# A two-layer decoder trunk in split fp32r: three of eight row-block pairs of the down products by seven products, in a new order

## The chip, the cores and the metric

The kernel runs on one core of a Trainium2 chip. The metric is the device time of one execution in microseconds (us). The core has a matrix engine (TensorE), a vector engine (VectorE), an activation engine (ScalarE), GpSimd, a queue of loads (SyncE) and 16 DMA engines. In the rows of the profile they are called PE (its weight loads PEld), DVE, ACT, POOL, SP. Each runs its own instructions in program order and waits on semaphores for the others.

## The reference

256 tokens of width 2048 pass through a gated mixer, a feed-forward block, an attention block and a second feed-forward block, all in float32. The change lies in the two feed-forward blocks:

```python
def swiglu_ffn(x, norm_g, w_gate, w_up, w_down):
    h = rms_norm(x, norm_g)                                   # 256 x 2048
    return (jax.nn.silu(h @ w_gate) * (h @ w_up)) @ w_down    # 5632 hidden columns
```

`x` and the result are 256 x 2048, `w_gate` and `w_up` 2048 x 5632, `w_down` 5632 x 2048.

## The kernel before

**Split products.** Each float32 matrix is written as hi + lo in the matrix engine's format fp32r. One product of a 128x128 block with 128x512 weights is three matmuls: hi by hi (L1609), hi by lo (L1610), lo by hi (L1611). ScalarE makes w_hi by a copy (L741). VectorE makes w_lo as raw - w_hi (`plain_lo`, L1160). Some half groups are "added" (table `ADDED`): ScalarE writes -raw to w_lo as well (L743), and GpSimd starts a transfer that adds raw to it in memory (L541), so VectorE has nothing to do for them.

**Half groups and pairs.** The 16 row blocks of a product are eight row-block pairs, numbered 0 to 7. For two column groups g and u (512 columns each) the plain way takes two half groups, g3 and u3 for instance, of 4 products (12 matmuls) each. The other way (`s0`) is a two-by-two block product in Winograd's form: 7 products (21 matmuls) in place of 8, over sums of blocks. `pair_sums` on VectorE (L1149, L1152, L1155, tile sums_b) forms the sums of the weights, `pair_hi` on ScalarE (L730) makes the three parts of s_hi, `pair_lo` on VectorE (L1165, L1168, L1171) the three parts of s_lo. The matrix engine waits for the first part (`blocks_split`) at the pair's start, and for the others 9 and 15 matmuls on. The left side's sums (`forms_begin`, `forms_next`, `forms_end`, `forms_hi_part`, `forms_lo_part`) are made once for a block.

**Stages.** The hidden columns go in parts (`PARTS`) of 4, 4 and 3 chunks. After the chunks of parts 0 and 1 come two blocks, "down 0" and "down 1", of two column groups each: 4 of each in the program. The third part has two plain columns and a "down middle" block.

**Order and memory.** `ORDERS` is written by hand and fixes the items' order on all engines; `ACT_ORDERS` is ScalarE's own where that differs. `LOADS` says which half groups share a load of 1 MB. A load goes to one of four slots of `raw`, in turn, and `slot_free` makes the load queue wait until the load four before it has been split: for a half group until w_lo is written, for an added one until its transfer is done, for a pair until s_lo is. w_hi and w_lo are rings of four half groups: ScalarE may write one when the matrix engine has used the one four before. s_hi and s_lo exist once; a part is rewritten when the pair before has used it. `hooks` are pieces of other work behind an item: `gate_sums` and `hidden` end the chunk before, `hidden_lo` (L983) splits its last columns.

Of the kernel before, what the change touches and what calls it, by code (L numbers as in the profile page):

```python
# [49 lines left out]
def yoco_kernel(nc, x, a_norm, a_w_in, a_ln_g, a_ln_b, a_w_s, a_b_s, a_w_out, kv_norm, w_k, w_v, k_norm,  # L50
# [24 lines left out]
    WINO, WINO_H = 4, 2  # L75
# [5 lines left out]
    def loads_of(text):  # L81
# [6 lines left out]
              "down 0": items("g2 g3 g4 g5 u2 u3 g6 g7 s0 u4 u5 s1 u6 u7"),  # L88
              "down 1": items("g2 g3 g4 g5 g6 g7 s0 u2 u3 u4 u5 s1 u6 u7"),
# [3 lines left out]
             "down 0": loads_of("g2 g3,g4 g5,u2 u3,g6 g7,s0,u4 u5,s1,u6 u7"),  # L93
             "down 1": loads_of("g2 g3,g4 g5,g6 g7,s0,u2 u3,u4 u5,s1,u6 u7"),
# [121 lines left out]
    with ExitStack() as ctx:  # L216
# [18 lines left out]
        junk_b = sb("junk_b", [P, CH], mybir.dt.bfloat16)  # L235
# [32 lines left out]
        with ExitStack() as part:  # L268
# [9 lines left out]
            f4_hi = sb("f4_hi", [P, WINO - 2, P], F32R, part)  # L278
            f4_lo = sb("f4_lo", [P, WINO - 2, P], F32R, part)
# [31 lines left out]
        def in_place(rows, first=0):  # L311
            return rows[:, first:first + 4:2, P:2 * P]
# [246 lines left out]
        def _(act):  # L559
# [187 lines left out]
            def forms_hi_part(n, dst, fourth, rest=None):  # L747

                act.wait_ge(forms_ready, n)
                pairs_n = dst.shape[1]  # L750
# [4 lines left out]
                ins.then_inc(forms_hi, 1)

            def feed_forward(layer, norm, last_save, last_lhs):
# [34 lines left out]
                for p, (c0, c1) in enumerate(PARTS):  # L792
                    for c in range(c0, c1):
                        k = layer, "chunk", c
                        if c == 0:
# [10 lines left out]
                    if p in DOWN_PAIRS:  # L806
                        block_hi((layer, "down", p, 0),
                                 {("g", 3): [lambda: read_p1(k)], ("g", 4): [lambda: silu(c1 - 1)],
                                  ("u", 2): [lambda: hidden_hi(c1 - 1, c0)],
                                  ("u", 3): [lambda: forms_hi_part(FORMS[layer, "down", p, 0], fh_hi, in_place(h_hi))]})  # L810
                        block_hi((layer, "down", p, 1), {("g", 3): [lambda: read_p1((layer, "down", p, 0))]})
                        continue
# [15 lines left out]
                    middle = {("g", 2): [lambda: forms_hi_part(FORMS[km], fh_hi, in_place(h_hi, h_spare(p)))]}  # L828
# [120 lines left out]
        def _(dve):  # L949
# [213 lines left out]
            def pair_lo(n, slot):  # L1163
# [708 lines left out]
```

## Time and profile before

| | us |
|---|---|
| median of 3 runs | 2074.83 (2074.07 to 2074.86) |
| the profiled execution | 2074.55 |
| its span, first to last instruction | 2072.8 |
| TensorE busy | 2065.6 (100%) |
| VectorE busy | 1672.9 (81%) |
| ScalarE busy | 1208.1 (58%) |

The rows carry times from the start of the span. A matmul's row shows 0.39 us, but the matmuls overlap, and the distance from one start to the next is what a matmul costs. VectorE's and ScalarE's rows overlap a little too, by about 0.1 us; lengths are therefore read from start to start.

### The profile page before, as it was taken

What the parts mean: (1) busy time and instruction counts of PE and PEld (TensorE: products, weight loads), DVE (VectorE), ACT (ScalarE), POOL (GpSimd) and SP (SyncE); (2) the same over time, 40 slices, a digit from 0 to 9 for tenths busy, and PEclk for the clock granted to TensorE, in tenths of its full rate; (3) what the DMA queues carried; (4) which work ended last, traced back from release to release, by engine and by line L of the source; (5) the groups of instructions that cost most, each with busy time, mean ns of one, the idle gap of its engine ahead of it and who ended that gap; (6) DMA issues with size and microseconds to landing.
All of it is one profiled execution on the core that took longest, in us unless ns stands there. A gap on an engine that the chain in (4) does not pass through costs nothing.

```text
span 2072.8 us, 24481 instructions
## 1 busy us (share of the span) xinstructions
PE 2065.6 (100%) x9394; PEld 1714.7 (83%) x9394; DVE 1672.9 (81%) x1847; ACT 1208.1 (58%) x1452; POOL 93.2 (4%) x107
## 2 busy tenths in 40 slices
PE   9999999999999999999999999999999999999999
PEld 8888888888888888888888888878888888888887
DVE  5466579999899998988566666579999899998987
ACT  6444556665566655656666665466665566655653
POOL 1000001000000000000011001001000000000000
PEclk9999999999999999999999999999999999999999
DMA  8655547875687767765555455447866687767764
GB/s 326 206 179 175 174 159 236 259 226 197 199 269 228 231 215 212 241 210 203 195 184 168 147 187 174 163 143 240 266 214 208 194 273 219 241 207 213 241 216 150
DMA packets 212255, 434.66 MB, mean 210 GB/s; under 512 B 9040, under 2 KB 9648, under 8 KB 211888
## 3 DMA queue, kind: packets, MB, share of 16 engines
q1 hardware_dynamic: 202720, 398.50, 57.5%
q0 software_dynamic: 9424, 34.65, 8.1%
q8 instruction: 74, 1.21, 0.2%
q14 instruction: 37, 0.30, 0.0%
HBM read 399.56 MB, written 2.10 MB: 194 GB/s over the span
## 4 chain that ended last, share of the span: by engine, by line
PE 97%; DVE 1%; ACT 1%; DMA 1%; issue 0%; POOL 0%; DVEq 0%; POOLq 0%; ACTq 0%
PE acc L1609 18%; PE acc L1610 18%; PE acc L1611 18%; PE acc L1468 11%; PE acc L1472 11%; PE acc L1470 11%; PE tr L1610 2%; PE tr L1609 2%; PE tr L1611 2%; PE tr L1516 1%; DMA w_lo<-raw 1%; PE tr L1789 0%; PE tr L1579 0%; PE tr L1763 0%; PE tr L1773 0%; PE acc L1525 0%
## 5 line engine op out<-in xcount | busy, mean ns | idle before, releaser
L741 ACT ACTIVATE w_hi<-raw 128x1024 fp32r<-128x1024 f32 x320 | 328.0, 1053 | 180.4 <-PE acc L1611 160.7
L1160 DVE TENSOR_TENSOR w_lo<-raw,w_hi 128x1024 fp32r<-128x1024 f32 x260 | 308.1, 1219 | 24.1 <-ACT w_hi L741 24.1
L1609 PE MATMUL acc<-w_hi,a_hi 128*128 128x512 f32 x736 | 288.2, 392 | 1.5 <-DVE w_lo L1160 1.3
L1611 PE MATMUL acc<-w_hi,a_lo 128*128 128x512 f32 x736 | 286.6, 389 | 0.0
L1610 PE MATMUL acc<-w_lo,a_hi 128*128 128x512 f32 x736 | 286.4, 389 | 0.0
L730 ACT ACTIVATE s_hi<-sums_b 128x1024 fp32r<-128x1024 f32 x208 | 213.0, 1054 | 97.9 <-DVE sums_b L1155 90.5
L1468 PE MATMUL acc<-w_hi,a_hi 128*128 128x512 f32 x640 | 254.7, 398 | 0.0
L1472 PE MATMUL acc<-w_hi,a_lo 128*128 128x512 f32 x640 | 249.7, 390 | 0.0
L1470 PE MATMUL acc<-w_lo,a_hi 128*128 128x512 f32 x640 | 249.2, 389 | 0.0
L961 DVE TENSOR_TENSOR w_lo<-raw,w_hi 128x1024 fp32r<-128x1024 f32 x127 | 154.9, 1237 | 116.1 <-ACT w_hi L579 116.0
L730 ACT ACTIVATE s_hi<-raw 128x1536 fp32r<-128x1536 f32 x104 | 154.5, 1486 | 140.6 <-PE acc L1611 140.6
L965 DVE SCALAR_TENSOR_TENSOR w_lo<-raw,gains,w_hi 128x512 fp32r<-128x512 f32 x192 | 134.5, 748 | 83.8 <-ACT w_hi L583 83.7
L579 ACT ACTIVATE w_hi<-raw 128x1024 fp32r<-128x1024 f32 x127 | 132.2, 1058 | 117.0 <-PE acc L1472 115.8
L1165 DVE TENSOR_TENSOR s_lo<-raw,s_hi 128x1536 fp32r<-128x1536 f32 x104 | 182.4, 1754 | 20.0 <-ACT s_hi L730 20.0
L1609 PE MATMUL acc<-w_hi,h_hi 128*128 128x512 f32 x448 | 174.7, 390 | 0.0
L1611 PE MATMUL acc<-w_hi,h_lo 128*128 128x512 f32 x448 | 174.3, 389 | 0.0
L1610 PE MATMUL acc<-w_lo,h_hi 128*128 128x512 f32 x448 | 174.3, 389 | 0.0
L1609 PEld LDWEIGHTS acc<-w_hi,a_hi 128*128 128x128 f32 x736 | 138.2, 188 | 30.3 <-issue 1.7
L1611 PEld LDWEIGHTS acc<-w_hi,a_lo 128*128 128x128 f32 x736 | 138.2, 188 | 28.9
L1610 PEld LDWEIGHTS acc<-w_lo,a_hi 128*128 128x128 f32 x736 | 138.2, 188 | 28.1
L583 ACT ACTIVATE w_hi<-raw,gains 128x512 fp32r<-128x512 f32 x192 | 126.1, 713 | 60.5 <-PE acc L1472 60.4
L1472 PEld LDWEIGHTS acc<-w_hi,a_lo 128*128 128x128 f32 x640 | 120.1, 188 | 25.5
(225 smaller groups left out, 3903.5 us busy)
## 6 DMA issues: line engine op xcount, KB each, us to landing
raw<-in_ffn_w_down_dram SPq DMA_DIRECT2D x68, 1024.0 KB, 5.1
raw<-in_ffn_w_gate_dram SPq DMA_DIRECT2D x46, 1024.0 KB, 5.6
raw<-in_ffn_w_up_dram SPq DMA_DIRECT2D x46, 1024.0 KB, 6.6
raw<-in_ffn_w_gate_dram SPq DMA_DIRECT2D x84, 512.0 KB, 4.0
raw<-in_ffn_w_up_dram SPq DMA_DIRECT2D x84, 512.0 KB, 5.4
raw<-in_a_w_in_dram SPq DMA_DIRECT2D x30, 1024.0 KB, 5.3
w_lo<-raw POOLq DMA_DIRECT2D x60, 512.0 KB, 8.2
raw<-in_ffn_w_down_dram SPq DMA_DIRECT2D x40, 512.0 KB, 5.1
```

The costliest lines, as they stand in the source:

```text
L730: nc.scalar.activation(s_hi[:, operands, :], src, ACT.Copy).then_inc(s_cast, 1)
L741: ins = nc.scalar.activation(w_hi[:, m % RING, :, :], src, ACT.Copy)
L961: nc.vector.tensor_tensor(lo, src, hi, ALU.subtract).then_inc(lo_split, 1)
L965: ins = nc.vector.scalar_tensor_tensor(out=lo[:, k, :], in0=src[:, k, :], scalar=gains[:, gain + kb:gain + kb + 1], in1=hi[:, k, :], op0=A ...
L1160: nc.vector.tensor_tensor(w_lo[:, m % RING, :, :], raw[:, slot, half * HG:(half + 1) * HG, :], w_hi[:, m % RING, :, :].bitcast(F32), ALU.s ...
L1165: nc.vector.tensor_tensor(s_lo[:, 0:3, :], raw[:, slot, 1:4, :], s_hi[:, 0:3, :].bitcast(F32), ALU.subtract)\
L1468: nc.tensor.matmul(acc[s][t][:, :], hi[:, kb, tok], w_hi[:, slot, k, :], start=kb == 0, stop=False)
L1470: nc.tensor.matmul(acc[s][t][:, :], hi[:, kb, tok], w_lo[:, slot, k, :], start=False, stop=False)
L1472: ins = nc.tensor.matmul(acc[s][t][:, :], lo[:, kb, tok], w_hi[:, slot, k, :], start=False, stop=kb == HG * n - 1)
L1609: nc.tensor.matmul(bank[:, :], hi, rhs_hi, start=start, stop=False)
L1610: nc.tensor.matmul(bank[:, :], hi, rhs_lo, start=False, stop=False)
L1611: return nc.tensor.matmul(bank[:, :], lo, rhs_hi, start=False, stop=stop)
```

## The change

`WINO_H` goes from 2 to 3, so pair 2 of a down block is done by seven products as well. The orders and loads of down 0 and down 1 are new, three half groups of each down 0 (g3, g4, u7) are added ones, and the hooks are hung elsewhere. Three small tiles are gone (junk_b and the two of f4): f4 now lies in the down blocks' forms, from which `place_fourth` copies it into a_hi and a_lo, and `save_chunk` writes its squares into `res` before the copy.

```diff
-    WINO, WINO_H = 4, 2
+    WINO, WINO_H = 4, 3
...
-              "down 0": items("g2 g3 g4 g5 u2 u3 g6 g7 s0 u4 u5 s1 u6 u7"),
-              "down 1": items("g2 g3 g4 g5 g6 g7 s0 u2 u3 u4 u5 s1 u6 u7"),
+              "down 0": items("g3 g4 g5 u3 u4 u5 s0 g6 s1 g7 s2 u6 u7"),
+              "down 1": items("g3 g4 g5 g6 s0 g7 u7 s1 u3 u4 s2 u5 u6"),
...
-             "down 0": loads_of("g2 g3,g4 g5,u2 u3,g6 g7,s0,u4 u5,s1,u6 u7"),
-             "down 1": loads_of("g2 g3,g4 g5,g6 g7,s0,u2 u3,u4 u5,s1,u6 u7"),
+             "down 0": loads_of("g3 u3,g4 g5,u4 u5,g6 g7,s0,u6 u7,s1,s2"),
+             "down 1": loads_of("g3 g4,g5 g6,s0,g7 u7,s1,u3 u4,s2,u5 u6"),
...
-    ADDED = {"chunk": items("g7 u4 u5"), "first": [], "down 0": [], "down 1": [], "down middle": []}
-    ACT_ORDERS = {"chunk": items("g4 g5 g6 g7 s0 u4 s1 u5 s2 s3 u6 u7")}
+    ADDED = {"chunk": items("g7 u4 u5"), "first": [], "down 0": items("g3 g4 u7"), "down 1": [], "down middle": []}
+    ACT_ORDERS = {"chunk": items("g4 g5 g6 g7 s0 u4 s1 u5 s2 s3 u6 u7"),
+                  "down 0": items("g3 g4 g5 u3 u4 u5 s0 g6 s1 g7 u7 s2 u6")}
...
+            def place_fourth(k):
+                act.wait_ge(w_used, HG_OF[k, ("u", 3)] + 1)
+                act.wait_ge(forms_hi, FORMS[k])
+                act.wait_ge(forms_lo, FORMS[k])
+                nc.scalar.activation(in_place(a_hi, 4), f4_hi.bitcast(F32), ACT.Copy)
+                nc.scalar.activation(in_place(a_lo, 4), f4_lo.bitcast(F32), ACT.Copy).then_inc(fourth_placed, 1)
...
-                        block_lo(k0, {("g", 3): [lambda: gate_sums(c1 - 1)], ("g", 4): [lambda: hidden(c1 - 1)],
-                                      ("g", 5): [lambda: dve.wait_ge(staged, b0 + c1 - NC),
-                                                 lambda: forms_begin(h_hi, h_lo, WINO_H, PAIRS_BEFORE[k0])],
-                                      ("u", 2): [lambda: forms_next(WINO_H), lambda: forms_end(WINO_H)],
-                                      ("u", 3): [lambda: hidden_lo(c1 - 1, c0),
-                                                 lambda: forms_lo_part(FORMS[k0], fh_hi, fh_lo, in_place(h_hi), in_place(h_lo))],
-                                      ("g", 7): [lambda: dve.wait_ge(forms_lo, FORMS[k0]), lambda: sums(k0, 0)], ("u", 5): [lambda: sums(k0, 1)]})
+                        block_lo(k0, {("g", 4): [lambda: gate_sums(c1 - 1)], ("g", 5): [lambda: hidden(c1 - 1)],
+                                      ("u", 3): [lambda: dve.wait_ge(staged, b0 + c1 - NC),
+                                                 lambda: forms_begin(h_hi, h_lo, WINO_H, PAIRS_BEFORE[k0])],
+                                      ("u", 4): [lambda: forms_next(WINO_H), lambda: forms_end(WINO_H)],
+                                      ("u", 5): [lambda: forms_lo_part(FORMS[k0], fh_hi[:, :, :], fh_lo[:, :, :],
+                                                                       in_place(h_hi, 0, WINO_H), in_place(h_lo, 0, WINO_H)),
+                                                 lambda: dve.wait_ge(forms_lo, FORMS[k0]), lambda: sums(k0, 0)],
+                                      ("g", 6): [lambda: sums(k0, 1)], ("g", 7): [lambda: sums(k0, 2)]},
+                                 {("s", 0): [lambda: hidden_lo(c1 - 1, c0)]})
...
-                        block_lo(k1, {("g", 3): [lambda: down_sums(p, 0), lambda: down_first(0)], ("g", 5): [lambda: down_second(p, 0)],
-                                      ("g", 7): [lambda: sums(k1, 0, added + 2)], ("u", 4): [lambda: sums(k1, 1)]})
+                        block_lo(k1, {("g", 4): [lambda: down_sums(p, 0)],
+                                      ("g", 6): [lambda: down_second(p, 0), lambda: sums(k1, 0, added + 1)],
+                                      ("s", 0): [lambda: down_first(0)],
+                                      ("u", 7): [lambda: sums(k1, 1)], ("u", 4): [lambda: sums(k1, 2)]})
```

VectorE in down 0 of the first layer's first part. Before, from s_lo of the pair s0 on:

```order
L1165 TENSOR_TENSOR s_lo<-raw,s_hi 128x1536
L1168 TENSOR_TENSOR s_lo<-sums_b,s_hi 128x1024
L1171 TENSOR_TENSOR s_lo<-sums_b,s_hi 128x1024
L1160 TENSOR_TENSOR w_lo<-raw,w_hi 128x1024 x2
L1149 TENSOR_TENSOR sums_b<-raw 128x1024
L1152 TENSOR_TENSOR sums_b<-sums_b,raw 128x512
L1155 TENSOR_TENSOR sums_b<-sums_b,raw 128x512
L1165 TENSOR_TENSOR s_lo<-raw,s_hi 128x1536
L1168 TENSOR_TENSOR s_lo<-sums_b,s_hi 128x1024
L1171 TENSOR_TENSOR s_lo<-sums_b,s_hi 128x1024
L1160 TENSOR_TENSOR w_lo<-raw,w_hi 128x1024 x4
```

In the change, from behind s_lo of s0 to the first part of s_lo of s2 (`pair_lo` stands on L1175 to L1183 there, `plain_lo` on L1170):

```order
L1170 TENSOR_TENSOR w_lo<-raw,w_hi 128x1024
L1159 TENSOR_TENSOR sums_b<-raw 128x1024
L1162 TENSOR_TENSOR sums_b<-sums_b,raw 128x512
L1165 TENSOR_TENSOR sums_b<-sums_b,raw 128x512
L1175 TENSOR_TENSOR s_lo<-raw,s_hi 128x1536
L1178 TENSOR_TENSOR s_lo<-sums_b,s_hi 128x1024
L1183 TENSOR_TENSOR s_lo<-sums_b,s_hi 128x1024
L1170 TENSOR_TENSOR w_lo<-raw,w_hi 128x1024
L1159 TENSOR_TENSOR sums_b<-raw 128x1024
L1162 TENSOR_TENSOR sums_b<-sums_b,raw 128x512
L1165 TENSOR_TENSOR sums_b<-sums_b,raw 128x512
L1175 TENSOR_TENSOR s_lo<-raw,s_hi 128x1536
```

Between two pairs stood two half groups (u4, u5); now stands one (g6, then g7), and the sums of the next pair are right behind it.

The load queue in the same block, with what each load waits for. Before (s0, u4 u5, s1, u6 u7):

```order
L421 DMA raw<-in_ffn_w_down_dram 128x2x512 [waits lo_split]
L422 DMA raw<-in_ffn_w_down_dram 128x2x512
L428 DMA raw<-in_ffn_w_down_dram 128x4x512 [waits lo_split]
L421 DMA raw<-in_ffn_w_down_dram 128x2x512 [waits lo_split]
L422 DMA raw<-in_ffn_w_down_dram 128x2x512
L428 DMA raw<-in_ffn_w_down_dram 128x4x512 [waits lo_split]
```

In the change (s0, u6 u7, s1, s2):

```order
L423 DMA raw<-in_ffn_w_down_dram 128x2x512 [waits lo_split,lo_added0]
L424 DMA raw<-in_ffn_w_down_dram 128x2x512
L430 DMA raw<-in_ffn_w_down_dram 128x4x512 [waits lo_split,lo_added1]
L423 DMA raw<-in_ffn_w_down_dram 128x2x512 [waits lo_split]
L424 DMA raw<-in_ffn_w_down_dram 128x2x512
L423 DMA raw<-in_ffn_w_down_dram 128x2x512 [waits lo_split]
L424 DMA raw<-in_ffn_w_down_dram 128x2x512
```

The last load of the block was a plain one behind the split of g7; now it is that of the pair s2, and it waits for the split of g7 too (the fourth load before it is `g6 g7`).

ScalarE in the same block, whose waits name the slots of `raw`. Before (u4 and u5, s1, u6 and u7):

```order
L741 ACTIVATE w_hi<-raw 128x1024 [waits w_used,raw_landed1] x2
L730 ACTIVATE s_hi<-raw 128x1536 [waits s_used,raw_landed2,s_landed2]
L730 ACTIVATE s_hi<-sums_b 128x1024 [waits s_used,s_sums]
L730 ACTIVATE s_hi<-sums_b 128x1024 [waits s_used]
L741 ACTIVATE w_hi<-raw 128x1024 [waits w_used,raw_landed3] x2
```

In the change (s1, g7, u7 with its negative, and the first part of s2):

```order
L732 ACTIVATE s_hi<-raw 128x1536 [waits s_used,raw_landed2,s_landed2]
L732 ACTIVATE s_hi<-sums_b 128x1024 [waits s_used,s_sums]
L732 ACTIVATE s_hi<-sums_b 128x1024 [waits s_used]
L743 ACTIVATE w_hi<-raw 128x1024 [waits w_used,raw_landed3]
L743 ACTIVATE w_hi<-raw 128x1024 [waits w_used,raw_landed1]
L745 ACTIVATE w_lo<-raw 128x1024
L732 ACTIVATE s_hi<-raw 128x1536 [waits s_used,raw_landed3,s_landed3]
```

The pair s1 came from slot 2, filled long before; now g7 and the pair s2 behind it are both read from slot 3.

## Rows read from the trace of the kernel before

**Rows 1.** The page, parts 1 and 2: busy time, granted clock by fortieths.
```profile
PE 2065.6 (100%) x9394; PEld 1714.7 (83%) x9394; DVE 1672.9 (81%) x1847; ACT 1208.1 (58%) x1452; POOL 93.2 (4%) x107
...
PEclk9999999999999999999999999999999999999999
```

**Rows 2.** Waits, TensorE: us in total, times, longest us.
```profile
PE acc L1525 <- POOL ident L496: 1.6, 1, 1.6
PE acc L1609 <- DVE w_lo L1160: 1.3, 1, 1.3
```

**Rows 3.** Timeline, TensorE, first down 0: start us, us, work, count.
```profile
457.05 0.39 PE L1609 MATMUL acc<-w_hi,h_hi 128*128 128x512 f32 x1
...
479.71 0.39 PE L1609 MATMUL acc<-s_hi,h_hi 128*128 128x512 f32 x1
...
484.47 0.39 PE L1609 MATMUL acc<-w_hi,h_hi 128*128 128x512 f32 x1
```

**Rows 4.** Timeline, VectorE, the same block.
```profile
452.44 0.69 DVE L1183 TENSOR_TENSOR sums_b<-acc,sums_b 128x512 f32<-128x512 f32 x1 [0.66 <-ACT sums_b L764]
...
456.36 1.22 DVE L1160 TENSOR_TENSOR w_lo<-raw,w_hi 128x1024 fp32r<-128x1024 f32 x1
457.49 1.22 DVE L1200 TENSOR_TENSOR sums_b<-acc,sums_b 128x1024 f32<-128x1024 f32 x1
...
459.96 1.22 DVE L1160 TENSOR_TENSOR w_lo<-raw,w_hi 128x1024 fp32r<-128x1024 f32 x1
...
463.36 0.42 DVE L1006 TENSOR_TENSOR sums_b<-form_a 128x256 f32<-128x256 f32 x1
...
465.63 1.23 DVE L1160 TENSOR_TENSOR w_lo<-raw,w_hi 128x1024 fp32r<-128x1024 f32 x1 [0.72 <-ACT w_hi L741]
466.78 1.28 DVE L983 TENSOR_TENSOR h_lo<-tr,h_hi 128x512 fp32r<-128x512 f32 x2
467.98 0.95 DVE L1020 TENSOR_TENSOR fh_lo<-sums_b,fh_hi 128x768 fp32r<-128x768 f32 x1
...
469.18 2.36 DVE L1160 TENSOR_TENSOR w_lo<-raw,w_hi 128x1024 fp32r<-128x1024 f32 x2
471.45 1.22 DVE L1149 TENSOR_TENSOR sums_b<-raw 128x1024 f32<-128x1024 f32 x1
...
474.04 1.75 DVE L1165 TENSOR_TENSOR s_lo<-raw,s_hi 128x1536 fp32r<-128x1536 f32 x1
475.70 1.22 DVE L1168 TENSOR_TENSOR s_lo<-sums_b,s_hi 128x1024 fp32r<-128x1024 f32 x1
...
477.97 2.35 DVE L1160 TENSOR_TENSOR w_lo<-raw,w_hi 128x1024 fp32r<-128x1024 f32 x2
```

**Rows 5.** Timeline, ScalarE, the same block.
```profile
445.30 3.89 ACT L741 ACTIVATE w_hi<-raw 128x1024 fp32r<-128x1024 f32 x4
...
463.57 1.09 ACT L609 ACTIVATE h_hi<-tr 128x512 fp32r<-128x512 f32 x2 [2.48 <-PE tr L1516]
...
465.49 0.85 ACT L751 ACTIVATE fh_hi<-sums_b 128x768 fp32r<-128x768 f32 x1
...
466.53 1.06 ACT L741 ACTIVATE w_hi<-raw 128x1024 fp32r<-128x1024 f32 x1
```

**Rows 6.** Line L541, all accumulating transfers.
```profile
DMA to landing us min/median/max: 4.3/8.2/10.7
```

**Rows 7.** Line L541 at 417.89, then at 432.98: one transfer each.
```profile
DMA to landing us min/median/max: 4.4/4.4/4.4
...
DMA to landing us min/median/max: 8.7/8.7/8.7
```

**Rows 8.** Line L422, second half of one pair's load: at 549.73, 593.15, 552.47.
```profile
DMA to landing us min/median/max: 4.6/4.6/4.6
...
DMA to landing us min/median/max: 6.1/6.1/6.1
...
DMA to landing us min/median/max: 8.6/8.6/8.6
```

More of the change, by code:

```diff
@@ L234, in yoco_kernel @@
         ident = sb("ident", [P, P], F32)
-        junk_b = sb("junk_b", [P, CH], mybir.dt.bfloat16)
         gains = sb("gains", [P, 6 * KB], F32)
@@ L307, in yoco_kernel, with in_place @@
         x_banks = [None, acc[2], acc[1], tr]
-        def in_place(rows, first=0):
-            return rows[:, first:first + 4:2, P:2 * P]
+        def in_place(rows, first=0, n=2):
+            return rows[:, first:first + 2 * n:2, P:2 * P]
+        f4_hi, f4_lo = fh_hi[:, 0:2, 0:P], fh_lo[:, 0:2, 0:P]
         def h_spare(p):
@@ L619, in save_chunk @@
                 act.wait_ge(staged, b + 1 - NC)
-                nc.scalar.activation(res[:, :, c * CH:(c + 1) * CH], stage[:, :, :], ACT.Copy)
-                step.inc(nc.scalar.activation(junk_b[:, :], stage[:, 0, :], ACT.Square,
-                                              accum_out=sums[:, n, 0, c:c + 1]))
+                saved = res[:, :, c * CH:(c + 1) * CH]
+                for t in range(TT):
+                    step.inc(nc.scalar.activation(saved[:, t, :], stage[:, t, :], ACT.Square,
+                                                  accum_out=sums[:, n, t, c:c + 1]))
                 step.wait()
-                nc.scalar.activation(junk_b[:, :], stage[:, 1, :], ACT.Square,
-                                     accum_out=sums[:, n, 1, c:c + 1]).then_inc(res_saved, 1)
+                nc.scalar.activation(saved, stage[:, :, :], ACT.Copy).then_inc(res_saved, 1)
             act.wait_ge(rows_transposed, 1)
@@ L807, in feed_forward @@
                         block_hi((layer, "down", p, 0),
[L808 to L811, printed above, removed]
+                                 {("g", 4): [lambda: read_p1(k)], ("g", 5): [lambda: silu(c1 - 1)],
+                                  ("u", 4): [lambda: hidden_hi(c1 - 1, c0)],
+                                  ("u", 5): [lambda: forms_hi_part(FORMS[layer, "down", p, 0], fh_hi[:, :, :],
+                                                                   in_place(h_hi, 0, WINO_H))]})
+                        block_hi((layer, "down", p, 1), {("g", 4): [lambda: read_p1((layer, "down", p, 0))]})
                         continue
@@ L827, in feed_forward @@
                     first = {1: [lambda: read_p1(k)], 2: [lambda: silu(c1 - 1)], 3: [lambda: hidden_hi(c1 - 1, c0)]}
-                    middle = {("g", 2): [lambda: forms_hi_part(FORMS[km], fh_hi, in_place(h_hi, h_spare(p)))]}
+                    middle = {("g", 2): [lambda: forms_hi_part(FORMS[km], fh_hi[:, 0:len(pairs(km)), :], in_place(h_hi, h_spare(p)))]}
                     last = {1: [lambda: read_p1(km)]}
@@ L1161, in plain_lo, with pair_lo @@
                                         w_hi[:, m % RING, :, :].bitcast(F32), ALU.subtract).then_inc(lo_split, 1)
-            def pair_lo(n, slot):
+            def pair_lo(n, slot, between=()):
                 dve.wait_ge(s_cast, n * 3 + 1)
@@ L1169, in pair_lo @@
                     .then_inc(t24_split, 1)
+                for work in between:
+                    work()
                 dve.wait_ge(s_cast, n * 3 + 3)
@@ L1247, in sums, with block_lo @@
                     pair_sums(PAIR_OF[k, q], slot, BOTH_OF[k, ("s", q)], before + count)
-                def block_lo(k, hooks):
+                def block_lo(k, hooks, between={}):
                     for item in order(k):
@@ L1252, in block_lo @@
                         if item[0] == "s":
-                            pair_lo(PAIR_OF[k, item[1]], slot)
+                            pair_lo(PAIR_OF[k, item[1]], slot, between.get(item, ()))
                         elif item not in ADDED[kind(k)]:
@@ L1318, in feed_forward @@
                              4: [lambda: dve.wait_ge(staged, b0 + c1 - NC),
-                                 lambda: forms_begin(h_hi, h_lo, WINO_H, PAIRS_BEFORE[km]), lambda: forms_next(WINO_H)],
-                             5: [lambda: forms_end(WINO_H)]}
-                    middle = {("g", 2): [lambda: forms_lo_part(FORMS[km], fh_hi, fh_lo, in_place(h_hi, h_spare(p)), in_place(h_lo, h_spare(p)))],
+                                 lambda: forms_begin(h_hi, h_lo, len(pairs(km)), PAIRS_BEFORE[km]),
+                                 lambda: forms_next(len(pairs(km)))],
+                             5: [lambda: forms_end(len(pairs(km)))]}
+                    middle = {("g", 2): [lambda: forms_lo_part(FORMS[km], fh_hi[:, 0:len(pairs(km)), :], fh_lo[:, 0:len(pairs(km)), :],
+                                                                        in_place(h_hi, h_spare(p)), in_place(h_lo, h_spare(p)))],
                               ("g", 4): [lambda: dve.wait_ge(forms_lo, FORMS[km]), lambda: sums(km, 0)],
@@ L1709, in feed_forward @@
                             waits = {("g", 4): [lambda: pe.wait_ge(gate_ready, NUMBER[layer, "chunk", c - 1] + 1)],
-                                     ("s", 0): [lambda: pe.wait_ge(staged, b0 + c - NC)]}
+                                     ("s", 0): [lambda: pe.wait_ge(staged, b0 + c - NC)],
+                                     ("s", 2): [lambda: pe.wait_ge(fourth_placed, layer + 1)]}
                             hooks = {("g", 5): [lambda: transpose_batch(b0 + c - 1)]}
```

41 lines of the change are left out of this document (19 added, 22 removed).

## The prediction, written before the changed kernel was run

> **What bounds the kernel now.** I read the page's busy time first, then TensorE's waits, then the timelines of one down 0 block. TensorE is busy for 2065.6 of 2072.8 us and its granted clock is at full speed in every fortieth [rows 1]. Its two largest waits are 1.6 us at the very start and 1.3 us for one w_lo [rows 2]. So the kernel is as long as its matmuls, and whatever comes late for a matmul is added in full. VectorE is the next engine (81%) [rows 1], and it makes s_lo, without which a pair can't begin. The question is what the 24 dropped matmuls give and what the new order makes late.
>
> In the block I follow, the first matmul starts at 457.05, the pair s0 at 479.71, the half group behind it at 484.47 [rows 3]. A pair of 21 matmuls takes 4.76 us, so 0.227 us a matmul and 2.72 us a half group of 12. The 22.66 us to the pair are eight half groups (21.78) and eight transposes (0.88).
>
> **What it removes.** In each of the 8 down blocks a third pair goes from 24 matmuls to 21: 24 x 0.227 = 5.4 us, all on the path. With no wait added the profiled execution of 2074.55 would become 2069.1.
>
> **down 0, laid out on the clock of that block.** Without waits TensorE would do: six half groups and the transposes from 457.05 to 474.25, s0 to 479.0, g6 to 481.7, s1 to 486.5, g7 to 489.2, then s2.
>
> *The added g3 and g4.* ScalarE copies four half groups from 445.30, 0.97 us each [rows 5]. The first two remain (u6, u7, to 447.2), then come g3 (448.2), its negative (449.1), g4 and its negative (about 451.8, its load lands near 450). VectorE's bank sums start at 452.44 behind ScalarE's read of the pair's product [rows 4], so the negatives just fit in front of that. The transfer of g3 is issued at about 449.4. One took 4.4 us where no load was in flight and 8.7 where one had just been issued [rows 7]; over all 60 it is 4.3 to 10.7 [rows 6]. Two 1 MB loads are in flight here, so I take 8.7: g3 lands at 458.1, where TensorE wants it at 457.05, **1.05 us late**. g4, issued at 452.05, lands at 460.75 and is wanted at 460.8. Bounds: no delay at 4.4, 3.05 at 10.7.
>
> The Trainium skill ("DMA: Bandwidth & Descriptors", "Anatomy of one DMA — SWDGE (gpsimd) path") fits a GpSimd transfer as about 2 us plus its bytes at 436 GB/s; its estimate for 0.5 MB would be 3.2 us, and g3 would land in time. By that rule the wait falls away and the sum is some 2 us lower. The trace speaks against it: its shortest transfer took 4.3 us, its median 8.2 [rows 6].
>
> *VectorE's chain to s0.* Bank sums to 456.36, split of g5 to 457.49, second sums and product to 459.96 [rows 4]. Split of u3 to 461.1 (1.13, as 456.36 to 457.49). form_a for three pairs is 1536 wide, as s_lo's first part, 474.04 to 475.70, 1.66 [rows 4]: 462.8. Split of u4: 463.9. The four small form sums took about 1.55 for two pairs (463.36 to 465.63, less 0.72 of idleness [rows 4]); half as much again for three gives 2.05: 465.95. ScalarE copies h_hi right behind the transposes [rows 5]; with 1.05 of delay this ends at 465.6, u5's copy at 466.5, the form copies (1.04 for two pairs [rows 5], 1.45 for three) at 468.0. VectorE then makes the forms' lo part (1.2 for two pairs [rows 4], 1.7 for three) to 469.75, the sums of s0 (471.45 to 474.04, 2.6) to 472.35, part one of s_lo to 474.0, part two to 475.15, hidden_lo (466.78 to 467.98, 1.2) to 476.35, part three to 477.5. TensorE wants them at 475.3, 477.3 and 478.7. Before, s_lo was whole at 477.97 and the pair started at 479.71; the six groups in place of eight use that lead up, but s0 isn't late.
>
> *s1.* Behind s0 VectorE has per pair and half group: split 1.13, sums 2.6, s_lo 3.93 (474.04 to 477.97 [rows 4]), together 7.66. TensorE takes 4.76 + 2.72 = 7.48. g6 is split at 478.6, the sums are ready at 481.2, part one at 482.9; TensorE stands at s1 at 482.8: **about 0.2 late**. s1 runs from 483.0 to 487.8, g7 to 490.5.
>
> *s2, the large term.* Its load goes into the slot of `g6 g7` and waits for the split of g7. This stands behind the last part of s1's s_lo: 485.15 + 1.13 = 486.3. It can't be sooner, since s_hi and s_lo exist once and s1's parts wait for s0's matmuls. The queue issues the two halves at 486.4 and 486.8. In the nearest rows a second half landed after 4.6, 6.1 and 8.6 us [rows 8]. u7's transfer is issued within half a microsecond of it, little else is in flight: I take 5.8, so 492.6. Only then can the sums be formed (495.2) and part one of s_lo (496.9). TensorE is at the pair at 490.5: **6.5 us of wait**. Bounds 5.3 (at 4.6) and 9.3 (at 8.6). All operations behind the waiting ones, ScalarE's s2 casts and the split of u6, are ready within the pair's own 4.76.
>
> Together 1.05 + 0.2 + 6.5 = 7.75 us a block; or s2 starts at 496.95 instead of 489.2, the same. Four down 0 blocks: 31 us.
>
> **down 1.** Counted from its start, VectorE's bank sums end at -0.7 (456.36 to 457.05 [rows 4, 3]), g5's split at 0.5, g6's, held by the ring until u7 is used and copied, at 2.4, second sums and columns at 5.0, the sums of s0 at 7.6, its first part at 9.3. TensorE wants it at 4 x 2.72 = 10.9. g7 follows at 14.1 (wanted 15.6), part one of s1 at 19.6 (21.1), of s2 at 28.4 (31.3); the load of s2 waits for s0's split (11.7), not for a group next to it. No wait, with 1.5 us to spare; if 2.0 were missing it would cost 0.5 a block, 2 in all.
>
> **Edits at nothing.** `place_fourth` adds two small copies a layer on ScalarE, 58% busy [rows 1], long before their reader (chunk 1's s2). `save_chunk` keeps its three operations in another order. The three additions a block relieve VectorE of 3 x 1.13 us, but not between s0 and s2, where no split is taken away. u7's transfer, 10.7 us at most [rows 6] from 487, ends before TensorE reaches it at 504.
>
> **Sum.** 2074.55 - 5.4 + 31 = 2100.1; the profiled execution stands 0.3 below the median of 2074.83, which changes nothing. I say **2100**.
>
> **Rivals.**
> 1. *The wait cools the array.* No wait of the trace is over 1.6 us and the clock never leaves the 2.4 GHz level [rows 1, 2], so what 6.5 us of idleness do isn't shown. If the granted clock then falls to 1.2 GHz, a matmul takes 0.454. Bounds: nothing, or the whole pair s2 at half pace, 4.76 more. The middle, 2.4, four times: 2100 + 9.6 = 2110.
> The Trainium skill ("TensorE: Matmul & The Clock Gate", "Part 1: The HAM clock gate") says an array left idle goes to 1.2 GHz and has to be kept busy to get back; by it this rival is what happens, and no run here shows it yet.
> 2. *The load is early enough, faster than before.* If s2's load were issued before g7's split (were the slot another), and the transfers landed in 4.4, all 5.4 us stay: 2069.1. It decides if g7 is split 6.5 us sooner. The order of loads speaks against it, each takes the next slot in turn. With the load early but g3 late and s1 0.2 late, 4 x 1.25 = 5 are lost: 2074.6, no change.
> 3. *Half the wait.* The load lands in 4.6 and VectorE has lead I don't see, so s2 waits 3 us: 2074.55 - 5.4 + 4 x 3.5 = 2083.
> 4. *Transfers crowd.* g3 at 10.7 moves the chain by about 2 us (the copies of h_hi wait for the transposes), the load at 8.6 adds 2.8: s2 starts at 501.7, 12.5 a block: 2119.
>
> **Chances.** Forecast 0.47, cooled array 0.35, half the wait 0.06, crowded 0.06, load early 0.06 (half of it faster, half no change). The low end of the forecast takes transfers of 4.4 (TensorE in time, the chain half a microsecond sooner) and a landing of 4.6: 6 us a block, 2093. The range runs from 2091 to 2117, past the cooled array's 2110 and short of the crowded case. A measurement tells 0.2%, 4 us, from no change. Faster 0.03, same 0.04, slower 0.93.
>
> **What would show it.** TensorE's waits: a group of four, 5 to 9 us each, for s_lo's first part, in the four down 0 blocks, with VectorE idle before it for a DMA of raw; the load queue waiting for VectorE's w_lo just ahead of that load; waits of about 1 us for w_lo<-raw transfers at the four starts; none in down 1. PEclk below 9 in fortieths around 490 us would show rival 1. The prediction is wrong if VectorE doesn't sit idle for raw in down 0, or if s2's load is issued before the split of g7.

## The result and the profile after

The changed kernel takes **2130.81 us** (median of 6, 2126.0 to 2134.0) against 2074.46 before (6 runs, 2074.0 to 2074.86): a ratio of **1.0271**, 95% interval 1.026 to 1.0282. Slower, as forecast, but above the range of 2091 to 2117.

The page's first part, to be held against [rows 1]:

```profile
PE 2077.1 (98%) x9370; PEld 1718.6 (81%) x9370; DVE 1696.8 (80%) x1867; ACT 1231.0 (58%) x1476; POOL 104.4 (5%) x119
```

TensorE runs 24 matmuls fewer and is busy for *longer*: 2077.1 us where 2065.6 - 5.4 = 2060.2 would do. That is 16.9 us more. About 14.0 of them are matmuls at half pace (the distances from start to start over 0.227 us, added up behind the seven waits that were followed by such matmuls). The other 3 or so are the restarts behind the waits, which the rows of e4 below show. The rest of the loss is in the waits themselves (us in total, times, longest), where [rows 2] had 1.6 and 1.3:

```profile
PE acc L1627 <- DVE s_lo L1175: 36.6, 8, 9.4
PE acc L1627 <- DMA w_lo<-raw: 7.8, 5, 2.0
PE acc L1543 <- POOL ident L498: 1.6, 1, 1.6
PE acc L1627 <- DVE w_lo L1170: 1.4, 1, 1.4
```

The two new groups, 44.4 us, all lie in the four down 0 blocks: s2 waits 9.4, 9.4, 8.2 and 8.4 us, s1 about 0.3 each, g3 1.90, 1.95, 1.82 and 1.75, and g4 once 0.34. Together 44.4 + 16.9 - 5.4 = 55.9, and the profiled executions differ by 2131.13 - 2074.55 = 56.6.

The first down 0 block is the one that was laid out. Its timeline for TensorE (start us, us, work, what it waited for), beside [rows 3]:

```profile
459.15 0.47 PE L1627 MATMUL acc<-w_hi,h_hi 128*128 128x512 f32 x1 [1.90 <-DMA w_lo<-raw]
...
460.41 0.63 PE L1629 MATMUL acc<-w_hi,h_lo 128*128 128x512 f32 x1
460.83 0.63 PE L1627 MATMUL acc<-w_hi,h_hi 128*128 128x512 f32 x1
...
486.04 0.50 PE L1627 MATMUL acc<-s_hi,h_hi 128*128 128x512 f32 x1 [0.31 <-DVE s_lo L1175]
...
503.23 0.80 PE L1627 MATMUL acc<-s_hi,h_hi 128*128 128x512 f32 x1 [9.41 <-DVE s_lo L1175]
503.82 0.63 PE L1628 MATMUL acc<-s_lo,h_hi 128*128 128x512 f32 x1
...
507.67 0.61 PE L1628 MATMUL acc<-s_lo,fh_hi 128*128 128x512 f32 x1
508.09 0.41 PE L1629 MATMUL acc<-s_hi,fh_lo 128*128 128x512 f32 x1
```

A matmul at half pace shows 0.63 us and starts 0.43 after the one before it, where 0.227 is the pace of before. There are 11 of them from 503.23 on, and 8 from 460.41 on (the last one shows 0.56), behind a wait of no more than 1.90. The page's row of the granted clock reads 9 in every fortieth, because a fortieth is 53 us long; so the sign that the prediction named for rival 1, PEclk below 9 around 490 us, did not appear although the rival came true. Short windows show the dips (us of window, busy time of PE, PEld, DVE, ACT, POOL, then granted clock, DMA share, GB/s):

```profile
457.00:460.00 3.00, 1.10 (x6) 0.75 (x5) 2.90 (x3) 1.06 (x1) 0.00 (x0) 1.00 1.08 246
460.00:464.00 4.00, 4.00 (x12) 3.16 (x11) 3.02 (x3) 0.30 (x1) 0.00 (x0) 0.57 0.68 167
...
495.00:500.00 5.00, 0.00 (x0) 0.00 (x0) 1.17 (x1) 1.22 (x1) 0.00 (x0) 0.79 0.98 310
...
503.00:508.00 5.00, 4.77 (x11) 3.80 (x12) 5.00 (x6) 3.39 (x4) 0.00 (x0) 0.50 0.03 7
```

0.50 is the level of 1.2 GHz. Before s2 the clock fell while TensorE sat idle: from 490 to 495, where TensorE's last matmul starts at 493.43, it is 1.00, from 495 to 500, with no matmul at all, it is 0.79 in the mean, and at s2's start it is 0.50. Behind g3's wait it fell only after TensorE had resumed: it is still 1.00 up to 460.

What s2 waits for is one step back, on VectorE (beside [rows 4]):

```profile
475.38 1.75 DVE L1175 TENSOR_TENSOR s_lo<-raw,s_hi 128x1536 fp32r<-128x1536 f32 x1
...
488.18 1.22 DVE L1170 TENSOR_TENSOR w_lo<-raw,w_hi 128x1024 fp32r<-128x1024 f32 x1
498.83 1.23 DVE L1159 TENSOR_TENSOR sums_b<-raw 128x1024 f32<-128x1024 f32 x1 [9.44 <-DMA raw<-in_ffn_w_down_dram]
...
501.43 1.75 DVE L1175 TENSOR_TENSOR s_lo<-raw,s_hi 128x1536 fp32r<-128x1536 f32 x1
```

VectorE splits g7 at 488.18, then sits idle for 9.4 us. The load queue shows why: the pair's load is issued when that split is done, and down 1's first load (L430) stands right behind it.

```profile
489.47 0.37 SPq L423 DMA_DIRECT2D raw<-in_ffn_w_down_dram  x1
489.89 0.46 SPq L424 DMA_DIRECT2D raw<-in_ffn_w_down_dram  x1
490.40 16.57 SPq L430 DMA_DIRECT2D raw<-in_ffn_w_down_dram  x2
```

GpSimd issues u7's accumulating transfer in the same instant, after g3's and g4's at the block's start:

```profile
449.51 0.87 POOL L543 DMA_DIRECT2D w_lo<-raw  x1 [15.65 <-ACT w_lo L745]
452.40 0.85 POOL L543 DMA_DIRECT2D w_lo<-raw  x1 [2.02 <-ACT w_lo L745]
489.50 0.86 POOL L543 DMA_DIRECT2D w_lo<-raw  x1 [36.24 <-ACT w_lo L745]
```

How long they took to land: first the load issued at 489.89, beside [rows 8], then the transfers of g3 and g4, beside [rows 7].

```profile
DMA to landing us min/median/max: 8.8/8.8/8.8
...
DMA to landing us min/median/max: 9.5/9.7/9.9
```

### The profile page after: what moved, and what is told of

Read it like the earlier page. It is cut to its first block, busy times and chain, and to the rows that moved or that the text cites. A ratio compares the mean times of both kernels' runs of the same rounds, so it can differ in the third digit from the quotient of the medians.

```text
span 2129.4 us, 24523 instructions
## 1 busy us (share of the span) xinstructions
PE 2077.1 (98%) x9370; PEld 1718.6 (81%) x9370; DVE 1696.8 (80%) x1867; ACT 1231.0 (58%) x1476; POOL 104.4 (5%) x119
## 3 DMA queue, kind: packets, MB, share of 16 engines
q1 hardware_dynamic: 202976, 398.50, 55.9%
## 4 chain that ended last, share of the span: by engine, by line
PE 82%; DVE 8%; DMA 6%; ACT 2%; issue 1%; SPq 0%; DVEq 0%; ACTq 0%
PE acc L1627 14%; PE acc L1628 14%; PE acc L1629 14%; PE acc L1486 10%; PE acc L1490 10%; PE acc L1488 10%; DMA raw<-in_ffn_w_down_dram 4%; PE tr L1629 2%; PE tr L1627 2%; PE tr L1628 2%; DMA w_lo<-raw 2%; PE tr L1534 1%; DVE s_lo L1175 1%; DVE sums_b L1159 1%; DVE w_lo L1170 1%
## 5 line engine op out<-in xcount | busy, mean ns | idle before, releaser
L743 ACT ACTIVATE w_hi<-raw 128x1024 fp32r<-128x1024 f32 x304 | 309.7, 1051 | 139.9 <-PE acc L1629 116.3
L732 ACT ACTIVATE s_hi<-sums_b 128x1024 fp32r<-128x1024 f32 x224 | 228.7, 1054 | 143.7 <-DVE sums_b L1165 136.9
L1170 DVE TENSOR_TENSOR w_lo<-raw,w_hi 128x1024 fp32r<-128x1024 f32 x232 | 274.4, 1217 | 18.0 <-ACT w_hi L743 18.0
L732 ACT ACTIVATE s_hi<-raw 128x1536 fp32r<-128x1536 f32 x112 | 166.5, 1487 | 175.3 <-PE acc L1629 139.3
L971 DVE TENSOR_TENSOR w_lo<-raw,w_hi 128x1024 fp32r<-128x1024 f32 x127 | 153.4, 1224 | 118.7 <-ACT w_hi L581 118.7
L1175 DVE TENSOR_TENSOR s_lo<-raw,s_hi 128x1536 fp32r<-128x1536 f32 x112 | 196.3, 1753 | 17.1 <-ACT s_hi L732 17.1
L581 ACT ACTIVATE w_hi<-raw 128x1024 fp32r<-128x1024 f32 x127 | 132.2, 1058 | 117.9 <-PE acc L1490 115.8
L1159 DVE TENSOR_TENSOR sums_b<-raw 128x1024 f32<-128x1024 f32 x112 | 136.8, 1222 | 37.8 <-DMA raw<-in_ffn_w_down_dram 35.5
L1629 PEld LDWEIGHTS acc<-w_hi,a_lo 128*128 128x128 f32 x736 | 138.2, 188 | 29.0
L1627 PE MATMUL acc<-w_hi,h_hi 128*128 128x512 f32 x384 | 152.4, 397 | 7.8 <-DMA w_lo<-raw 7.8
L1629 PE MATMUL acc<-w_hi,h_lo 128*128 128x512 f32 x384 | 151.6, 395 | 0.0
L1628 PE MATMUL acc<-w_lo,h_hi 128*128 128x512 f32 x384 | 151.1, 394 | 0.0
```

The lines of the kernel that those rows point to most:

```text
L732: nc.scalar.activation(s_hi[:, operands, :], src, ACT.Copy).then_inc(s_cast, 1)
L743: ins = nc.scalar.activation(w_hi[:, m % RING, :, :], src, ACT.Copy)
L971: nc.vector.tensor_tensor(lo, src, hi, ALU.subtract).then_inc(lo_split, 1)
L1159: nc.vector.tensor_tensor(sums_b[:, 0:2, :], raw[:, slot, 0:1, :].to_broadcast([P, 2, CH]), raw[:, slot, 1:3, :], ALU.subtract).then_inc(s ...
L1170: nc.vector.tensor_tensor(w_lo[:, m % RING, :, :], raw[:, slot, half * HG:(half + 1) * HG, :], w_hi[:, m % RING, :, :].bitcast(F32), ALU.s ...
L1175: nc.vector.tensor_tensor(s_lo[:, 0:3, :], raw[:, slot, 1:4, :], s_hi[:, 0:3, :].bitcast(F32), ALU.subtract)\
```

## The experiments

Each is the changed kernel with the edit shown.

**e1: only the loads in another order.** The load of s2 takes the slot of s0, which is free much sooner than that of `g6 g7`. Three transfers a block stay.

```diff
-             "down 0": loads_of("g3 u3,g4 g5,u4 u5,g6 g7,s0,u6 u7,s1,s2"),
+             "down 0": loads_of("g3 u3,g4 g5,u4 u5,s0,g6 g7,s1,u6 u7,s2"),
```

> Only the order of down 0's eight loads differs from the changed kernel: g3 u3, g4 g5, u4 u5, s0, g6 g7, s1, u6 u7, s2. The load of pair s2 then takes the slot of s0 instead of that of g6 g7 and can be issued some 9 us sooner. Slot theory (the long wait is s2's load held until g7 is split): the waits of 9.4 us before s2 and the half-speed matmuls behind them go, 9.4 + 2.4 us a block, four times; left are the late g3 (1.9 us, plus 1.6 of half-speed matmuls) and 0.3 before s1: about 2085 us. Rival, VectorE (its work between s0 and s2 is what is too long and the load only coincides): s2 waits on for several us, above 2110 us. Rival, transfers (the load is slow because of the crowd, whenever it is issued): waits of 3 to 4 us before s1 or s2, about 2100 us.

Measured 2085.11 (2081.98 to 2086.84), ratio 1.0052 (1.0035 to 1.0068). Of the 56.3 us by which the change is slower, 45.7 are gone by one line that changes no work. In the first block the load goes out at 479.42, and VectorE runs from g7's split to s2's sums without a gap:

```profile
486.55 1.22 DVE L1170 TENSOR_TENSOR w_lo<-raw,w_hi 128x1024 fp32r<-128x1024 f32 x1
487.69 1.22 DVE L1159 TENSOR_TENSOR sums_b<-raw 128x1024 f32<-128x1024 f32 x1
```

What is left is mostly the transfers at the block's start (TensorE's waits):

```profile
PE acc L1627 <- DMA w_lo<-raw: 8.9, 7, 2.9
...
PE acc L1627 <- DVE s_lo L1175: 1.2, 4, 0.3
```

So the slot of `g6 g7` is the cause of the wait for s2 and of the cooling behind it: in the profile of e1 no s2 waits 0.25 us or more, and no half-pace matmuls stand behind one. That the total meets the forecast of 2085 so closely is in part luck: the forecast has half-pace matmuls behind each late g3, and the profile shows them behind one of four, while the restarts behind the waits were not counted.

**e2, e3, e5: fewer accumulating transfers, the loads as in the change.** e2 has none in down 0, e3 only g3 and g4, e5 only u7 (ScalarE's order `... g7 s2 u6 u7` in e2 and e3, since u7 needs no early copy there).

```diff
-    ... "down 0": items("g3 g4 u7"), ...
+    ... "down 0": [], ...                  # e2
+    ... "down 0": items("g3 g4"), ...      # e3
+    ... "down 0": items("u7"), ...         # e5
```

> The changed kernel with no added half groups in down 0: VectorE splits g3, g4 and u7 itself, and ScalarE takes u7 behind u6. Slot theory: g3 is in time (no 1.9 us wait and no slow matmuls behind it), the chain to g7's split is 3 us earlier, but s2's load still waits for that split; with u7's transfer gone it lands in 5.5 us in place of 8.9. Left per block: 1.0 before s1, 5.8 before s2, up to 2.4 of half-speed matmuls: 2106 us. Rival (the added transfers are the cause of it all): no wait before s2, about 2074 us. Rival (VectorE is the bound and three more splits make it worse): above 2131 us.

> The changed kernel with u7 of down 0 split by VectorE; g3 and g4 remain added. If u7's transfer, issued at the same time as s2's load, is what makes that load take 8.9 us instead of 5 to 6, the wait before s2 falls from 9.4 to about 6, with the rest as it is: 2118 us. If the 1 MB load issued right behind it is the crowd, nothing changes: 2131 us.

> The changed kernel with g3 and g4 split by VectorE; only u7 is added. The wait for g3 (1.9 us) and the eight half-speed matmuls behind it (1.6) go, s1 waits 1.0 in place of 0.3, and the chain to g7's split is about 3 us earlier while TensorE is 3.5 us earlier too, so the wait before s2 stays near 9.5: about 2121 us. If instead the late g3 costs nothing in the end because s2 waits for VectorE anyway, whose chain is bound to g3 only by ScalarE's ring: 2131 us.

| | us | ratio (95%) | waits for s_lo, us | waits for w_lo<-raw, us | s2's load lands after, first block |
|---|---|---|---|---|---|
| the change | 2130.81 | 1.0271 (1.026 to 1.0282) | 36.6 | 7.8 | 8.8 |
| e3, without u7 | 2121.12 | 1.022 (1.0203 to 1.0237) | 26.5 | 8.8 | 5.5 |
| e5, without g3, g4 | 2120.52 | 1.0221 (1.0204 to 1.0238) | 39.2 | none | 8.8 |
| e2, without all three | 2110.36 | 1.0176 (1.0159 to 1.0193) | 29.4 | none | 5.3 |

The last column as the trace prints it, for e3, e5 and e2:

```profile
DMA to landing us min/median/max: 5.5/5.5/5.5
```
```profile
DMA to landing us min/median/max: 8.8/8.8/8.8
```
```profile
DMA to landing us min/median/max: 5.3/5.3/5.3
```

In e3 the same 1 MB load still stands right behind the pair's (issued at 488.33, the next at 488.85), and the landing is 5.5. So it is u7's transfer that stretches it to 8.8 in the first block, not the load behind. The blocks differ: with the transfer the four landings are 8.8, 8.9, 7.6 and 7.8 in the change and 8.8, 7.9, 8.8 and 8.0 in e5, without it 5.5, 5.4, 6.9 and 5.3 in e3 and 5.3, 5.4, 6.5 and 5.9 in e2. In the third block the change and e3 are only 0.7 apart; what makes that landing longer without a transfer stays open.

By the medians u7's transfer costs 9.7 us, those of g3 and g4 10.3, and all three 20.4: they add up. Expected were 2118 for e3, 2121 for e5 and 2106 for e2. e5 met it. e3 came out 3 us higher, with waits for w_lo<-raw 1.0 longer than in the change and a wait of 7.4 for s2 in its third block. e2 came out 4 us higher: s2 waits 5.9, 6.0, 7.1 and 6.4 us where 5.8 were taken, and the restarts behind nine waits were not counted. Without any of the transfers the wait for s2 is still there: the slot is the main cause.

**e4: both edits, the loads of e1 and no added half group (ScalarE's order as in e2).**

> Both repairs: s2's load in the slot of s0, and no added half groups in down 0. If the two causes (the slot, the late g3) are the whole loss, what is left is VectorE's pace alone: 0.4 before s0, 1.0 before s1, some 0.3 before s2 per block, no half-speed matmuls: 2069.4 + 7 = 2076 us, even with the kernel before. If something else in the new order costs (down 1, the copies of the fourth forms), 2082 or more. If the 24 matmuls come back in full, 2069.

Measured 2075.51 (11 runs, 2074.27 to 2077.72) against 2074.1 in the same runs, 1.0007 (0.9998 to 1.0016): no difference that can be told. With both causes out, the third pair of products gives back no more than it costs. TensorE's waits, and then its busy time, say where its 5.4 us go: 3.5 of waits, and 2062.1 - 2060.2 = 1.9 more of busy time.

```profile
PE acc L1627 <- DVE s_lo L1175: 3.5, 4, 0.9
```
```profile
PE 2062.1 (99%) x9370; PEld 1708.8 (82%) x9370; DVE 1710.5 (83%) x1879; ACT 1220.7 (59%) x1464; POOL 93.4 (5%) x107
```

The 1.9 us are not matmuls at half pace: the mean granted clock is 1.000 in every one of the 11 runs, and no row behind a wait shows half pace. They are restarts. The rows at s1 in the first block:

```profile
481.65 0.39 PE L1629 MATMUL acc<-w_hi,h_lo 128*128 128x512 f32 x1
482.87 0.50 PE L1627 MATMUL acc<-s_hi,h_hi 128*128 128x512 f32 x1 [0.83 <-DVE s_lo L1175]
483.20 0.40 PE L1628 MATMUL acc<-s_lo,h_hi 128*128 128x512 f32 x1
```

From 481.65 to 482.87 are 1.22 us, which is the pace of 0.227, the wait of 0.83 and 0.16 more, and the next start comes after 0.34, another 0.11. So a wait costs some 0.3 us beyond its length even at full clock; four of them make 1.2, and small delays at the start of s2 make up most of the rest.

Without transfers VectorE is 0.9 us late at each s1, since only one half group (2.72 us of TensorE) stands between the pairs. In the first block the first part of s_lo starts at 472.21 for s0 and at 481.06 for s1, 8.85 us apart, where TensorE's pair and half group take 4.76 + 2.72 = 7.48; 1.2 of the 8.85 are `hidden_lo`, which the new hooks put between the parts of s0's s_lo. From s1 to s2 it is 7.67. The total met the forecast of 2076, but not term by term: no waits of 0.4 before s0 and 0.3 before s2 came, and the restarts, which were not in the sum, took the place of part of them.

**e6: does the cooling cost what the half-pace rows say?** 36 matmuls on a tile of zeros, which GpSimd fills at the start of the program, stand before s2 and fill the wait; they add nothing to the sums.

```diff
+            def fill(n):
+                for _ in range(n):
+                    nc.tensor.matmul(acc[1][0][0:96, 0:P], zero[:, 0:96], ident[:, :], start=False, stop=False)
...
+                            ("s", 2): [lambda: fill(36)]},
```

> The changed kernel with 36 short matmuls (zeros, added to a bank, 7.9 us in all) in front of pair s2 of each down 0, in the time in which TensorE would sit idle. The wait is set by s2's s_lo and stays. Clock theory (an idle TensorE is taken down to the lower clock and runs the first matmuls behind the wait at half pace): the 11 slow matmuls behind each long wait go, about 2.4 us a block, 2121 us; those behind the late g3 stay. If the slow rows come from something else (the bank, the memory behind the late load): 2131 us, with the slow rows still behind s2's start.

Measured 2123.48 (2123.11 to 2125.47), ratio 1.024 (1.0225 to 1.0256), 7.3 us less than the change though it does more. TensorE's timeline, in which the 36 matmuls are 72 rows merged into one:

```profile
493.89 8.02 PE L1677 MATMUL acc<-ident,edge_high 128*96 128x128 f32 x72
503.37 0.50 PE L1628 MATMUL acc<-s_hi,h_hi 128*128 128x512 f32 x1 [1.46 <-DVE s_lo L1176]
503.70 0.39 PE L1629 MATMUL acc<-s_lo,h_hi 128*128 128x512 f32 x1
```

and the window behind it:

```profile
503.00:506.00 3.00, 2.63 (x11) 2.17 (x12) 3.00 (x4) 3.00 (x4) 0.00 (x0) 1.00 0.00 0
```

s2 starts when it did (503.37, 503.23 in the change), but at full clock. Its 21 matmuls take 4.90 us up to the start of u6 (508.27), and 7.16 in the change (510.39): half pace behind s2 cost 2.3 us in this block, as the 11 rows say. Over the four blocks the rows of the change have 2.4, 2.4, 2.7 and 2.0 us of half pace behind s2. The medians show less, 7.3 / 4 = 1.8 us a block, but they do not compare this alone: in e6's profile the waits for g3 and s2 (the filling counted in) are some 2 us longer in all, and half-pace matmuls stand behind two of the late g3 where the change has them behind three.

**e7 and e8: two other layouts.** Both have e1's loads. e7 makes g6 the added half group, which takes a split off VectorE where it is late, ahead of s1; its transfer is issued at 469.08 in the first block, 9.2 us before TensorE comes to g6 at 478.33. e8 has none added, puts two half groups between s0 and s1, and gives ScalarE the same order.

```diff
+    ... "down 0": items("g6"), ...                                           # e7
+                  "down 0": items("g3 g4 g5 u3 u4 u5 g6 s0 s1 g7 s2 u6 u7")}  # e7, ScalarE's order
...
-              "down 0": items("g3 g4 g5 u3 u4 u5 s0 g6 s1 g7 s2 u6 u7"),
+              "down 0": items("g3 g4 g5 u3 u4 u5 s0 g6 g7 s1 u6 s2 u7"),      # e8
-                                      ("g", 6): [lambda: sums(k0, 1)], ("g", 7): [lambda: sums(k0, 2)]},
+                                      ("g", 7): [lambda: sums(k0, 1)], ("u", 6): [lambda: sums(k0, 2)]},
```

> As the version with both repairs, but g6 of down 0 is the one added half group, and ScalarE takes it ahead of s0, where it has 3 us of idleness. VectorE then has 1.13 us less between s0 and s1. VectorE theory: the 1.0 before s1 and 0.3 before s2 go; g6's transfer, issued near 471, lands by 475.5 to 480 for a use at 479, so up to 1 us of wait in its place: 2071 to 2075 us. If the transfer meets the loads of u6 u7 and takes 9 us or more: 2076 us or above, with waits for w_lo<-raw.

> As the version with both repairs, but down 0 in the order g3 g4 g5 u3 u4 u5 s0 g6 g7 s1 u6 s2 u7: two half groups between s0 and s1, only one behind s2. VectorE theory: no wait before s1 and s2 (7.66 us of VectorE against 10.2 of TensorE, then 7.66 against 7.48 with a lead), 0.4 before s0; but with one group behind s2 the bank sums end some 0.8 us after u7, so down 1's g3 waits for the bank: together 1.2 us a block, 2074 us. If the waits before s1 weren't VectorE's pace, they stay and the total is above 2078.

e7: **2071.2** (11 runs, 2070.6 to 2073.11), ratio 0.9988 (0.9979 to 0.9997). It is 2.9 us faster than the kernel before (2074.1 in the same runs), where the full gain would be 5.4, and 59.6 faster than the change. The interval lies below 1, but the gain is only 0.12%. Its page:

```profile
PE 2060.6 (100%) x9370; PEld 1708.0 (83%) x9370; DVE 1705.1 (82%) x1875; ACT 1224.4 (59%) x1468; POOL 97.4 (5%) x111
```

TensorE's busy time, 2060.6, is within 0.4 us of the 2060.2 that 24 matmuls fewer should give. Of s_lo's waits one of 0.3 us is left. Where the rest of the 5.4 us stays was not followed up. The transfer, with only the second half of one 1 MB load's flight beside it (issued at 466.49, landed 5.1 us later), landed in 5.0 us:

```profile
DMA to landing us min/median/max: 5.0/5.0/5.0
```

e8: 2074.0 (11 runs, 2072.8 to 2075.66), ratio 0.9999 (0.999 to 1.0008), no difference that can be told, as expected. The late s1 is gone, and another wait has come, for the bank sums in front of down 1:

```profile
PE acc L1627 <- DVE stage L1199: 2.7, 4, 0.7
```

## Why the prediction was off

The direction and the main mechanism held: s2's load behind the split of g7, VectorE idle for it, four long waits. The sizes were off, all upward: 62.0 us were lost in the four blocks (56.6 + 5.4), 15.5 a block, where 31 and 7.75 were reckoned. Two steps of the prediction failed. It left the fall of the clock out of the sum, and it took 5.8 us for a landing that took up to 8.8. The terms over the four blocks, from the profile of the change:

| | reckoned, us | measured, us |
|---|---|---|
| waits for s2 | 26.0 | 35.4 |
| waits for g3 (and once g4) | 4.2 | 7.8 |
| waits for s1 | 0.8 | 1.2 |
| matmuls at half pace | 0 | 14.0 |
| restarts behind the waits, and the rest | 0 | 3.6 |
| together | 31.0 | 62.0 |

- **24 matmuls, -5.4.** Right: e7's busy time is 2060.6 where 2060.2 was due.
- **g3 late by 1.05.** g3 starts at 459.15 where 458.1 was reckoned, 2.1 us late, of which the profile counts 1.90 as wait; in the four blocks the waits are 1.75 to 1.95. The transfer was issued at 449.5, as reckoned, but landed after 9.5, not 8.7. By the fit of the Trainium skill ("DMA: Bandwidth & Descriptors", "Anatomy of one DMA — SWDGE (gpsimd) path"), an estimate of 3.2 us for this size, it would have been in time. The trace does not agree: 9.5.
- **The chain to s0.** s_lo's first part at 475.38 where 472.35 was reckoned. 1.05 are g3's extra delay, and about 1.7 the eight half-pace matmuls, which put off the transposes and with them h_hi: ScalarE's copy of h_hi ends at 468.4 where 465.6 was reckoned. s0 itself wasn't late, the lead swallowed it, but everything behind it on VectorE was: g7's split came at 488.18 and not at 485.15.
- **s1 late by 0.2.** 0.3.
- **The landing of s2's load, 5.8.** The first step that failed: it was 8.8 in the first block and 7.6 to 8.9 in the four. The prediction saw that u7's transfer starts within half a microsecond and still counted "little else in flight". e3 and e5 show that this one transfer is worth 3.3 us of landing there. The trace of the kernel before had the answer: of the three loads of [rows 8] it is the one of 552.47, landing after 8.6, that has an accumulating transfer right in front of it, and the three like it in that trace (803.62, 1639.17, 1890.33) landed after 8.8, 7.8 and 9.0.

```profile
552.32 0.85 POOL L541 DMA_DIRECT2D w_lo<-raw  x1 [6.62 <-ACT w_lo L743]
```

s2 started at 503.23 and not at 496.95, 6.3 us later: about 3.1 from the chain and 3.0 from the landing. The chain put off TensorE's own arrival at s2 just as much, so the landing alone made the wait longer, 9.4 where 6.5 was reckoned.

- **The clock.** The second step that failed, and the larger one: the sum has it at nothing, it was only rival 1, at 0.35. It happened behind every s2 (9.4 us of half pace in the four blocks) and behind three of the four late g3 (4.6 us), together 14.0. The price named in the rival, 2.4 us behind s2, came out (2.0 to 2.7), but with luck: it was the middle between nothing and the whole pair. Half pace behind g3 was not reckoned anywhere. The Trainium skill ("TensorE: Matmul & The Clock Gate", "Part 1: The HAM clock gate") says that an array left idle goes to 1.2 GHz. Behind the long waits the trace agrees: 0.50 granted from 503 to 508.
- **down 1 without waits, u7 in time.** Right, there are none.
- **Rivals.** "Half the wait" and "load early" fell. "Transfers crowd" had the load's landing right (8.6) and took g3's too long (10.7 for 9.5). With the 9.6 of rival 1 added to its 2119 the sum would be 2129, close to what came, but by luck: 12.5 us of waits a block are too many (11.1 were measured) and 2.4 of half pace too few (3.5). Nothing in the prediction joins the two, although a load that lands later makes the idleness longer in which the clock falls. The landings could be read from the trace of before; the price of the clock could not, since its profile shows no idleness of this length.

What stays open: the short waits do not always cool the array. The late g3 of the four blocks, with the half-pace matmuls behind it:

| | waits, us | half-pace matmuls |
|---|---|---|
| the change | 1.90, 1.95, 1.82, 1.75 | 8, 8, 8, 0 |
| e1 | 1.73, 1.99, 1.63, 2.86 | 0, 0, 0, 7 |
| e3 | 2.11, 1.91, 2.32, 2.50 | 0, 8, 8, 7 |
| e6 | 1.98, 2.01, 1.77, 2.73 | 8, 0, 0, 8 |

That is 9 of 16: all four waits of 2.3 to 2.9 us and five of the twelve shorter ones. Among the shorter ones the length alone doesn't decide it: 1.82 was followed by half pace and 2.11 was not. The spread of the runs (8 us in the change, 0.9 before) goes with it, for the mean granted clock is on record for every run, not only for the profiled ones. In the change the clock is 0.987 in the two longest runs (2134.0, 2133.45), 0.988 in the next two (2131.13, 2130.48) and 0.990 in the two shortest (2129.62, 2126.0). In e1 it goes 0.997, 0.998, 0.999, 1.000 for 2086.84, 2085.88, 2084.35 and 2081.98. Before it is 1.000 in all.

## What to carry to other kernels

With slots taken in turn, the order of the loads decides what a load waits for: look at the item four loads back and at when it is used, not at how many slots there are. A transfer from memory to memory that starts with a load isn't free for the load, even when nobody waits for the transfer itself: before a landing is estimated, look at what else was issued beside the rows that it is taken from. And where TensorE is the bound, a wait costs more than its length: here some 0.3 us for the restart, and behind all 16 waits of 5.9 to 9.4 us matmuls at half pace. A change that saves 5 us has to be laid out so that hardly a wait arises.

## What the runs showed of the hardware

- A pair's load of two times 512 KB landed 5.3 to 6.9 us after its second half was issued when a 1 MB load stood behind it (e2, e3), and after 7.6 to 8.9 with one 0.5 MB accumulating transfer issued 0.4 us ahead of the second half as well (the change, e5). In the first blocks it landed after 5.3 and 5.5 with that load behind it (e2, e3) and after 5.0 and 5.2 without (e1, e4), so the load behind made little difference there.
- An accumulating transfer took 4.8 to 5.0 us in e7, beside the end of one 1 MB load, and 8.6 to 9.9 in the change, when two of them and loads were in flight.
- A wait of TensorE cost some 0.3 us beyond its length at full clock (e4: 0.83 us of wait, 0.27 more in the first two starts behind it).
- Behind 9.4 us of idleness 11 matmuls ran at the level of 1.2 GHz (the change, first block). Behind a wait of 1.9 us five matmuls ran at full pace and then 8 at half pace; behind seven other waits of 1.6 to 2.1 us none ran at half pace. Matmuls on zeros in the idle time kept the clock at 1.00 (e6).
